# A hybrid decoder layer on one core: first block's experts handed over in two halves, weight lines read in pairs without a packed copy

## The chip, the cores and the metric

The kernel runs on one core of a Trainium2 chip. The metric is the device time of one launch in microseconds (us), as the median of several runs. Its engines are TensorE (PE, with its weight loads shown apart as PEld), VectorE (DVE), ScalarE (ACT), GpSimd (POOL) and SyncE (SP). DMAs are issued from the queues of SP (all dense loads), POOL (the gathers) and ACT (the output), and run on 16 shared DMA engines.

## What is computed

One layer on x (1024 tokens x 1024 features, f32). Three residual branches follow each other:

```python
h = rmsnorm(x, norm_mix);   x = x + hybrid_mixer(h, ...)             # MLA, RG-LRU and differential attention
h = rmsnorm(x, norm_cross); x = x + memory_cross_attention(h, rmsnorm(mem, norm_mem), w_cq, w_ckv, w_co)
h = rmsnorm(x, norm_ffn);   x = x + peer_ffn(h, peer_w_q, peer_keys, peer_u, peer_v)
return rmsnorm(x, norm_final)
```

The last branch retrieves experts. Each token has 8 heads; each head scores two sets of 128 keys, takes the 16 best of each, adds them pairwise and takes the 16 best sums. This makes 128 experts per token:

```python
act = gelu(einsum('td,thkd->thk', xt, u[et]))       # a row of peer_u (4 KB) for each token and expert
y = einsum('thk,thkd->td', gt * act, v[et])         # and a row of peer_v (4 KB)
```

So 1024 tokens x 128 experts x 2 rows x 4 KB = 1073.7 MB have to be gathered from memory.

## The kernel before

**Blocks.** The tokens are worked through in 8 blocks (0 to 7) of 128, one token per partition. A block has a front end (norm, projections, attentions, recurrence, mixer output, cross-attention, queries, key scores, choice of experts) and 128 positions of expert work. At position p VectorE multiplies the gathered `u` row of expert p with the token's h (`multiply_row`, L2052, out to `dots`), ScalarE makes the activation and a diagonal matrix of it, and TensorE sums diagonal times `v` row into `ps_sum` (L1267); every eighth `v` row is added by VectorE instead (L2074). The front end of block b runs between the positions of block b-1. Which piece stands between which positions is written in tables by hand, `TENSOR_STOPS`, `VECTOR_STOPS` and `SCALAR_STOPS`, one entry per loop body: a number is the count of positions of block b-1 that the engine issues before it goes on with that part of the piece. Each body runs once (`LOOPS`). Ahead of the bodies stands an opening: the front end of block 0, which has no expert work under it, with the projection of the memory (`mem_piece`) and the five projections of block 1 (`next_0` to `next_4`) in it.

**Gathers.** POOL issues one indirect DMA for each of the 128 experts of a block and each table: 128 rows of 4 KB, 512 KB. The `u` rows go into a ring of 9 slots and the `v` rows into another of 9 (`retrieve`, L810 and L824). The order is fixed: 12 `u` gathers, and from then on one `u` and one `v` in turn, so that a `u` gather that waits for its slot (freed by `multiply_row`) also holds the `v` gathers behind it. The first 64 expert numbers of a block are handed over by `hand_first_ids` as soon as `choose_0` has them.

**The choice** is VectorE work in four pieces: `top_0` and `choose_0` for heads 0 to 3, `top_1` and `choose_1` for heads 4 to 7 (L1931 to L1998). In the opening `next_norm` (scale x of block 1, L1724; gains on its transpose, L1742) stands between `top_0` and `choose_0`. After `choose_1` the hand-over follows: second half of the numbers (L2011), the token's h (`h_cur`, L2015, in PSUM), the gates (L2022) and x (L2031). Only then comes the first body.

**Weights.** All dense weights lie in memory as `wstream`, slices of 128 x 512 numbers, 256 KB each. SP loads them two at a time into a ring of 4 pairs (`load_pair`, L601). Partition p needs line p of both slices, so a pair is read as two lines of 2 KB per partition. While the opening runs, `pack` (L607) also copies the 49 pairs of a block from memory to memory into `packed`, where the two lines stand side by side; block 1 and the later ones read `packed`, one run of 4 KB per partition. A block needs 49 pairs. The copies stand in SP's queue ahead of the pairs of the memory projection (two copies each, 32 in all), at `cross_scores` (12) and at `top_0` (5).

**Waits on counts.** Where VectorE waits for a count that grows with the block (`wait_more`), the value comes from a register: one instruction (L583) and a register addition, which the listing of the program's order shows as `ISA` and `REGISTER_ALU`.

## Time and profile before

| | |
|---|---|
| Median of 3 runs | 3484.84 us |
| Lowest, highest | 3477.87, 3487.18 us |
| Profiled execution: span from first to last instruction | 3488.4 us (the page gives no other time for this execution) |
| Instructions | 34790 |
| PE / PEld busy | 2948.9 us (85%) / 1651.9 us (47%) |
| DVE busy | 2349.6 us (67%) |
| ACT busy | 812.5 us (23%) |
| POOL busy | 2015.7 us (58%) |
| DMA | 1345.09 MB, mean 386 GB/s |
| Share of 16 DMA engines: POOL's gathers / SP's loads | 78.1% / 20.0% |

The page cuts the span into 40 slices of 87 us. Its row `DMA` is the busy share of the 16 DMA engines in tenths, its row `GB/s` what they moved. A view by windows gives the same numbers for chosen stretches; there a share of a little over 1 stands for full. The chain of waits is the chain that ended last, in order of time. `PEclk` is the granted clock of TensorE, 1.00 for 2.4 GHz and 0.50 for 1.2 GHz.

### The profile page before, as it was taken

How to read it: one execution, taken by the hardware profiler on the slowest of the kernel's cores; microseconds unless marked ns; L12 is line 12 of the kernel's file. 1: busy time of each engine (PE TensorE's matmuls, PEld its weight loads, DVE VectorE, ACT ScalarE, POOL GpSimd, SP SyncE). 2: the span in 40 equal slices, each digit the busy share in tenths (PEclk: the TensorE clock that was granted, in tenths of full speed). 3: DMA queues.
4: the chain of work that ended last, by engine and by line, in shares of the span. 5: the costliest groups of instructions: out<-in, count | busy, mean ns of one | idle time of the engine just before them, and what ended most of it. 6: DMA issues, size and time to landing. Idle time of an engine off the chain costs nothing.

```text
span 3488.4 us, 34790 instructions
## 1 busy us (share of the span) xinstructions
PE 2948.9 (85%) x10984; PEld 1651.9 (47%) x10984; DVE 2349.6 (67%) x5893; ACT 812.5 (23%) x1915; POOL 2015.7 (58%) x2085
## 2 busy tenths in 40 slices
PE   7876898888988898889997899888998889976675
PEld 6465455544545355534554456444564445522222
DVE  6229846886588765886578765886648865596555
ACT  3111411132211421133211322114221232211111
POOL 1004755666566765666565655665556655477775
PEclk9898999999999999999999999998999999999998
DMA  7788999999999999999999999999999999999998
GB/s 279 277 274 313 408 409 409 408 409 409 409 407 406 394 409 409 408 407 382 409 409 408 392 356 409 409 409 348 359 409 409 409 355 342 385 404 410 409 409 347
DMA packets 386971, 1345.09 MB, mean 386 GB/s; under 512 B 41762, under 2 KB 44834, under 8 KB 386148
## 3 DMA queue, kind: packets, MB, share of 16 engines
q0 software_dynamic: 294912, 1073.87, 78.1%
q1 hardware_dynamic: 90724, 264.79, 20.0%
q10 hardware_dynamic: 1152, 4.19, 0.3%
q8 instruction: 90, 1.47, 0.2%
q14 instruction: 93, 0.76, 0.1%
HBM read 1332.99 MB, written 35.39 MB: 392 GB/s over the span
## 4 chain that ended last, share of the span: by engine, by line
PE 38%; DMA 30%; DVE 15%; POOL 9%; issue 6%; ACT 3%; SPq 1%; DVEq 0%; POOLq 0%; ACTq 0%
PE ps_sum L1267 18%; DMA rows<-in_peer_u,ids_u 13%; DMA rows<-in_peer_v,ids_v 10%; PE ps_p L999 5%; POOL rows L824 5%; POOL rows L810 4%; DVE rows L2052 4%; PE ps_s L1181 4%; DMA rows<-in_peer_v,ids_u 3%; DMA w_ring<-packed 3%; PE ps_s L1118 2%; PE ps_p L1126 2%; DVE feat_b L1935 1%; DVE feat_b L1931 1%; PE ps_s L1114 1%
## 5 line engine op out<-in xcount | busy, mean ns | idle before, releaser
L1267 PE MATMUL ps_sum<-rows,diag 128*128 128x512 f32 x3548 | 1727.6, 629 | 267.1 <-DMA rows<-in_peer_v,ids_v 141.4
L2052 DVE CUSTOM_DVE_ANT_0 rows<-h_cur,rows 128x1024 f32<-128x1024 f32 x1024 | 1226.8, 1220 | 496.3 <-DMA rows<-in_peer_u,ids_u 483.3
L810 POOL DMA_INDIRECT rows<-in_peer_u,ids_u x1024 | 1012.3, 989 | 702.0 <-issue 483.3
L1267 PEld LDWEIGHTS ps_sum<-rows,diag 128*128 128x128 f32 x3548 | 671.0, 200 | 1155.7 <-issue 1005.7
L824 POOL DMA_INDIRECT rows<-in_peer_v,ids_v x512 | 490.3, 958 | 433.8 <-PE ps_sum L1267 277.6
L824 POOL DMA_INDIRECT rows<-in_peer_v,ids_u x512 | 498.2, 973 | 284.7 <-PE ps_sum L1267 144.2
L1528 ACT ACTIVATE diag<-ident,acts 128x128 f32<-128x128 f32 x887 | 324.7, 394 | 1049.4 <-PE ps_sum L1267 750.1
L999 PE MATMUL ps_p<-hT,w_ring 128*128 128x128 f32 x2944 | 358.7, 282 | 28.8 <-DMA w_ring<-packed 15.3
L999 PEld LDWEIGHTS ps_p<-hT,w_ring 128*128 128x128 f32 x2944 | 353.0, 198 | 61.2 <-issue 39.7
L1834 DVE CUSTOM_DVE_ANT_0 e<-ps_s,bias_t 128x256 f32<-128x256 f32 (+6 forms) x96 | 74.2, 773 | 176.3 <-PE ps_s L1118 73.7
L2074 DVE SCALAR_TENSOR_TENSOR x_cur<-rows,acts,x_cur 128x1024 f32<-128x1024 f32 x137 | 175.6, 1282 | 7.4 <-DMA rows<-in_peer_v,ids_v 7.3
L1905 DVE TENSOR_TENSOR x_next<-x_next,ps_s 128x512 f32<-128x512 f32 x32 | 21.9, 685 | 200.0 <-PE ps_s L1181 200.0
L1516 ACT ACTIVATE acts<-dots 128x8 f32<-128x8 f32 x128 | 26.6, 208 | 486.9 <-DVE dots L2052 486.6
L1181 PE MATMUL ps_s<-w_ring,hT 128*128 128x512 f32 x256 | 118.3, 608 | 14.2 <-DMA w_ring<-packed 7.4
L1441 ACT ACTIVATE e<-e,small 128x256 f32<-128x256 f32 (+6 forms) x96 | 75.4, 785 | 219.7 <-DVE small L1836 219.4
L999 PE MATMUL ps_p<-pT,w_ring 128*128 128x128 f32 x1024 | 118.8, 276 | 0.9 <-DMA w_ring<-packed 0.9
L999 PEld LDWEIGHTS ps_p<-pT,w_ring 128*128 128x128 f32 x1024 | 116.9, 192 | 5.4 <-issue 3.3
L1181 PE MATMUL ps_s<-w_ring,feat_b 128*128 128x512 f32 x256 | 114.8, 592 | 1.1 <-DMA w_ring<-in_wstream 1.1
L1935 DVE FIND_INDEX8 feat_b<-feat_b,e 128x8 uint32<-128x128 f32 (+1 forms) x384 | 103.4, 279 | 0.0
L1118 PE MATMUL ps_s<-k_diff,feat_a 32*128 32x512 f32 (+2 forms) x192 | 83.7, 543 | 16.9 <-DVE small L1836 16.8
L1314 ACT ACTIVATE feat_a<-ps_p 128x512 f32<-128x512 f32 (+2 forms) x48 | 26.0, 542 | 304.6 <-PE ps_p L999 304.5
L2052 DVE DVE_READ_ACCUMULATOR2_ANT dots<- 128x1 f32 x1024 | 84.4, 82 | 0.0
(288 smaller groups left out, 2376.2 us busy)
## 6 DMA issues: line engine op xcount, KB each, us to landing
w_ring<-packed SPq DMA_DIRECT2D x343, 512.0 KB
w_ring<-in_wstream SPq DMA_DIRECT2D x65, 512.0 KB
packed<-in_wstream SPq DMA_DIRECT2D x49, 512.0 KB, 8.2
rows<-in_peer_u,ids_u POOLq DMA_INDIRECT x1024, 14.9
rows<-in_peer_v,ids_u POOLq DMA_INDIRECT x512, 12.6
rows<-in_peer_v,ids_v POOLq DMA_INDIRECT x512, 19.3
bias_rows<-rows SPq DMA_DIRECT2D x5, 1024.0 KB, 12.1
bias_t<-in_x SPq DMA_DIRECT2D x8, 512.0 KB, 7.9
```

The costliest lines, as they stand in the source:

```text
L810: pool.indirect_dma_start(u_rows[:, slot, :], None, peer_u, bass.IndirectOffsetOnAxis(ap=ids_u[:, j:j + 1], axis=0)).then_inc(u_landed[slo ...
L824: pool.indirect_dma_start(v_rows[:, slot, :], None, peer_v, bass.IndirectOffsetOnAxis(ap=ids[:, j:j + 1], axis=0)).then_inc(v_landed[slot] ...
L999: ins = pe.matmul(dst, w[:, k, :], lhs[:, kt, :], start=(kt == 0), stop=(kt == KT - 1))
L1118: ins = pe.matmul(ps_s[:, c0:c1], q_diff[r:r + DK, half // 4, :], k_diff[r:r + DK, half // 4, c0:c1], start=True, stop=True)
L1181: pe.matmul(ps_s[:, n * 512:(n + 1) * 512], lhs[:, kt, :], w, start=(kt == 0), stop=(kt == KT - 1)).then_inc(w_used, 1)
L1267: ins = pe.matmul(ps_sum[:, c * 512:(c + 1) * 512], diag[:, n % 4, :], v_rows[:, slot, c * 512:(c + 1) * 512], start=(j == 0), stop=(n == ...
L1441: act.activation(buf[:, 0:keys_n], buf[:, 0:keys_n], ACT.Exp, bias=small[:, 32 + n:33 + n], accum_out=small[:, 48 + n:49 + n]).then_inc(s_ ...
L1528: act.activation(diag[:, n % 4, :], ident[:, :], ACT.Copy, scale=coef[:, j:j + 1]).then_inc(diag_made, 1)
L1834: run(dve.tensor_tensor_reduce(buf[:, 0:keys_n], ps_s[:, 0:keys_n], bias[:, 0:keys_n], 1.0, -3.0e38, ALU.add, ALU.max, small[:, 16 + n:17 ...
L1935: dve.max_index(i[:, first:first + 8], v[:, first:first + 8], s).then_inc(top_step, 1)
L2052: dve.tensor_tensor_reduce(row, h_cur[:, :], row, 1.0, 0.0, ALU.mult, ALU.add, dots[:, p:p + 1]).then_inc(u_used, 1)
L2074: dve.scalar_tensor_tensor(x_cur[:, :], v_rows[:, slot, :], coef[:, j:j + 1], x_cur[:, :], ALU.mult, ALU.add)\
```

## The change

1. `pack` and `packed` are gone. `load_pair` reads `wstream` directly, but so that partition (h, q) receives lines 2q and 2q+1 of slice h: one run of 4 KB. The features of the input thereby stand in another order in the partitions (`as_given` and `as_read` are the two orders of a row of 1024). Four pairs of a block, those of the recurrence's channels (`WHOLE`), are still read as two lines of 2 KB.
2. The order of features is made where rows are written: VectorE's writes of `feat_a`, `x_next`, `x_cur`, the scaled memory and `h_cur` step through one side with a stride, in 2 or 4 instructions for one. TensorE's transposes of `xs` and its products with `mem_v` read every second column. The gains (`cols`) come in 15 small DMAs for one.
3. In the opening `next_norm` no longer stands ahead of `choose_0`; `first_choose` does choose_0, the gates of the first half, scale, h, gains of block 1 and x. `top_1` and `choose_1` of block 0 become `late_top` and `late_choose`, the first pieces of the first body.
4. The transposes and gains of the first half of a row are no longer made in the middle of the output product, but both halves after it (`norm`).
5. VectorE's waits on registers become waits on constants (`wait_for`).
6. The tables of the first body are new; in the others one stop of `mix_out` and one of `cross_out` goes.

```diff
 TENSOR_STOPS = [
-    {"latents": (1,), "mla_up": (9,), "gates": (17, 18), "recur": (20, 26), "mla_0": (29, 30, 31), "mla_1": (31, 31, 32),
...
+    {"latents": (4,), "mla_up": (10,), "gates": (17, 18), "recur": (20, 26), "mla_0": (29, 30, 33), "mla_1": (33, 33, 33),
...
 VECTOR_STOPS = [
+    {"late_top": (0, 0, 0, 0, 0, 0), "late_choose": (0, 0, 0, 0, 0, 0, 0, 0, 1, 7, 7), "latents": (7, 7), "mla_up": (9,),
...
-                dst = w_ring[:, slot_of(n), :]
-                if n < MEM_SLICES + BLOCK_SLICES:
-                    dst, src = dst.rearrange("p (s c) -> p s c", s=2), wstream[i:i + 2].rearrange("s p c -> p s c")
+                dst, src = w_ring[:, slot_of(n), :], wstream[i:i + 2]
+                if i - MEM_SLICES in WHOLE:
+
+                    dst, src = dst.rearrange("p (s c) -> p s c", s=2), src.rearrange("s p c -> p s c")
+                elif 2 * KT <= i < MEM_SLICES:
+
+                    turn = (i - 2 * KT) % KT
+                    src = wstream[i - turn:i - turn + KT].rearrange("(h k) (q s) c -> k h q (s c)", h=2, s=2)[turn // 2]
                 else:
-                    src = packed[(i - MEM_SLICES) // 2]
+                    src = src.rearrange("h (q s) c -> (h q) (s c)", s=2)
                 sp.dma_start(dst, src).then_inc(w_landed[slot_of(n)], 16)
 
-            def pack(first, last):
...
-            sp.dma_start(cols[:, :], columns).then_inc(cols_in, 16)
             sp.dma_start(x_in[:, :], x[0:P, :]).then_inc(x_landed, 16)
+            sp.dma_start(cols[:, GAINS:COL["yn"]], columns[:, GAINS:COL["yn"]]).then_inc(cols_in, 16)
+            sp.dma_start(cols[:, COL["yn"] + KT:], columns[:, COL["yn"] + KT:]).then_inc(cols_in, 16)
+            for h in range(2):
+                own = slice(h * P // 2, (h + 1) * P // 2)
+                for n in range(4):
+                    sp.dma_start(cols[own, n * KT:(n + 1) * KT].rearrange("q (s k) -> q s k", s=2),
...
+                for n in (0, KT - 2):
+                    sp.dma_start(cols[own, COL["yn"] + n:COL["yn"] + n + 2],
...
+            sp.dma_start(cols[:, COL["yn"] + 2:COL["yn"] + KT - 2], columns[:, COL["yn"] + 2:COL["yn"] + KT - 2]).then_inc(gains_in, 16)
...
-                    pack(i - 1, i + 1)
...
-            def first_next(b):
-                sp.wait_ge(first_packed, 16 * IN_TILES)
-                front_loads(1, 0, per_tile * 3)
...
-                        if n == 1 and kt == 4:
-                            turn_added(b, norm, 0)
...
                 pace.part(0.6)
-                turn_added(b, n, 1)
+                for g in range(2):
+                    turn_added(b, n, g)
...
+            def wait_for(semaphore, waited, n):
+
+                waited[0] += n
+                dve.wait_ge(semaphore, waited[0])
...
-                dve.tensor_scalar(feat_a[:, :], x_in[:, :], small[:, 7:8], None, ALU.mult).then_inc(scaled, 1)
+                for n in range(2):
+                    ins = dve.tensor_scalar(as_read(feat_a)[:, n], as_given(x_in)[:, n], small[:, 7:8], None, ALU.mult)
+                ins.then_inc(scaled, 1)
...
+            def hand_row(b, ins_of):
+
+                for n in range(2):
+                    for half in range(2):
+                        ins = dve.scalar_tensor_tensor(as_given(h_cur)[:, n, :, :, half], as_read(x_next)[:, n, :, :, half],
+                                                       small[:, 105:106], as_given(ps_s)[:, n, :, :, half], ALU.mult, ALU.mult)
+                ins_of(ins)
...
+            def first_choose():
+
+                choose(0, 0)
+                scale_x(1)
+                dve.wait_ge(consts_in, 96)
+                dve.wait_ge(pre["v_out"], 4)
+                dve.wait_ge(ffn_spread, 1)
+                hand_row(0, steps.note)
+                dve.tensor_copy(g_cur[:, 0:FIRST], g_next[:, 0:FIRST]).then_inc(g_handed, 1)
+                for g in range(2):
+                    gain_x(1, 0, g)
+                hand_x(0)
+                steps.settle(dve)
+
+            def late_choose():
+
+                choose(0, 1)
+                dve.tensor_copy(ids_u[:, FIRST:], ids_next[:, FIRST:]).then_inc(ids_handed, 1)
+                dve.tensor_copy(g_cur[:, FIRST:], g_next[:, FIRST:]).then_inc(g_handed, 1)
+                dve.wait_ge(g_handed, 2)
+                hand_last_ids(0)
+                dve.wait_ge(v_ids_handed, 1)
+                dve.nop().then_inc(handed, 1)
```

**Where instructions move, VectorE, end of the opening.** Before, behind the last part of `choose_1` (`ids_u` are the expert numbers, the row of `h_cur,rows` is one position):

```order
L1990 TENSOR_REDUCE pT<-e 128x64
L1991 SCALAR_TENSOR_TENSOR pT<-pT 128x64
L1996 TENSOR_REDUCE small<-pT 128x8
L1997 RECIPROCAL small<-small 128x8
L1998 TENSOR_TENSOR pT<-pT,small 128x128
L2011 COPY ids_u<-pT 128x64
L2015 SCALAR_TENSOR_TENSOR h_cur<-x_next,small,ps_s 128x1024
L2022 COPY g_cur<-pT 128x128
L2026 COPY ids_v<-ids_u 128x64
L2031 COPY x_cur<-x_next 128x1024
L2127 UNCONDITIONAL_BRANCH
L1754 TENSOR_TENSOR pT<-feat_a 128x384
```

Changed, behind the last part of `choose_0`; what follows the branch is `late_top`:

```order
L2040 COPY ids_u<-pT 128x64
L2033 TENSOR_REDUCE small<-pT 128x4
L2034 RECIPROCAL small<-small 128x4
L2035 TENSOR_TENSOR pT<-pT,small 128x64
L1756 TENSOR_SCALAR feat_a<-bias_t,small 128x4x64x2 x2
L2046 SCALAR_TENSOR_TENSOR h_cur<-x_next,small,ps_s 128x256 x4
L2066 COPY g_cur<-pT 128x64
L1776 TENSOR_TENSOR hT<-ps_p,cols 128x512 x2
L2095 COPY x_cur<-x_next 128x512 x2
L2192 UNCONDITIONAL_BRANCH
L1963 MAX feat_b<-e 128x8 x8
```

The hand-over of h and x stands ahead of the second half's choice, and the scale and gains of block 1 (`feat_a`, `hT`) behind the first half's numbers instead of ahead of them.

**VectorE, where the positions begin.** Changed, in the middle of `late_choose`:

```order
L2020 TENSOR_TENSOR e<-pT,iota_f 128x1024
L2023 TENSOR_TENSOR e<-e,feat_b 128x1024
L2025 TENSOR_REDUCE pT<-e 128x64
L2118 ISA rows,dots<-h_cur,rows 128x1024
L2118 ISA dots 128x1
L2020 TENSOR_TENSOR e<-pT,iota_f 128x1024
L2118 ISA rows,dots<-h_cur,rows 128x1024
```

Before position 0 stand all of `late_top` and the greater part of `late_choose`; positions 1 to 6 follow one instruction later, and the last two large instructions of the choice stand behind position 6.

**SP, where the memory projection's weights are loaded.** Before:

```order
L683 DMA bias_t<-bias_rows 128x256
L607 DMA packed<-in_wstream 256x1x512 x2
L601 DMA w_ring<-in_wstream 128x2x512
L607 DMA packed<-in_wstream 256x1x512 x2
L601 DMA w_ring<-in_wstream 128x2x512
```

Changed:

```order
L701 DMA bias_t<-bias_rows 128x256
L615 DMA w_ring<-in_wstream 128x1024 x4
L615 DMA w_ring<-in_wstream 128x1x1024 x8
L692 ISA
```

The copies are gone from between the loads, and a load has 4 KB per partition in one run.

## Rows read from the trace of the kernel before

**Rows 1.** Page, part 2 and part 6: busy share and rate in 40 slices; the copies.

```profile
DMA  7788999999999999999999999999999999999998
GB/s 279 277 274 313 408 409 409 408 409 409 409 407 406 394 409 409 408 407 382 409 409 408 392 356 409 409 409 348 359 409 409 409 355 342 385 404 410 409 409 347
...
packed<-in_wstream SPq DMA_DIRECT2D x49, 512.0 KB, 8.2
```

**Rows 2.** By windows: start:end length, busy us of PE, PEld, DVE, ACT, POOL, clock, DMA share, GB/s.

```profile
86.00:96.00 10.00, 8.68 (x43) 7.32 (x41) 4.52 (x16) 0.00 (x0) 0.00 (x0) 0.98 1.05 398
198.00:213.00 15.00, 7.86 (x42) 7.02 (x42) 2.77 (x7) 4.68 (x12) 0.00 (x0) 0.77 1.01 318
252.00:262.00 10.00, 3.42 (x15) 2.86 (x15) 8.14 (x40) 0.00 (x0) 0.00 (x0) 0.59 0.05 18
306.00:340.00 34.00, 20.00 (x52) 11.28 (x52) 30.89 (x66) 5.81 (x15) 20.77 (x22) 0.66 0.82 289
340.00:1120.00 780.00, 678.66 (x2546) 383.25 (x2547) 549.83 (x1413) 188.73 (x467) 490.88 (x505) 0.95 1.03 409
2000.00:3060.00 1060.00, 950.54 (x3620) 539.19 (x3620) 708.45 (x1742) 270.37 (x597) 617.91 (x632) 0.95 0.98 382
```

**Rows 3.** Timeline of SP's queue: start, us of issue, line, what.

```profile
0.76 0.41 SPq L610 DMA_DIRECT2D cols<-in_columns  x1
...
2.63 3.07 SPq L601 DMA_DIRECT2D w_ring<-in_wstream  x4
```

**Rows 4.** Chain of waits, start and us of a piece.

```profile
6.74 9.76 DMA xs<-in_mem
...
57.21 14.46 DMA bias_rows<-rows
...
76.04 6.41 DMA w_ring<-in_wstream
```

**Rows 5.** Timeline of PE; in brackets the idle time before and its releaser.

```profile
82.49 7.41 PE L959 MATMUL h_cur<-rows,w_ring 128*128 128x256 f32 x24 [8.15 <-DMA w_ring<-in_wstream]
...
212.61 10.54 PE L1181 MATMUL ps_s<-w_ring,feat_b 128*128 128x512 f32 x24 [1.08 <-DMA w_ring<-in_wstream]
...
260.71 23.54 PE L999 MATMUL ps_p<-hT,w_ring 128*128 128x128 f32 x192 [0.78 <-DVE hT L1742]
...
298.21 2.05 PE L1018 MATMUL ps_p<-w_ring,hT 128*128 128x128 f32 x16 [0.45 <-DMA w_ring<-packed]
```

**Rows 6.** Timeline of VectorE from the end of `top_0` to the first body.

```profile
257.15 0.75 DVE L1724 TENSOR_SCALAR feat_a<-bias_t,small 128x1024 f32<-128x1024 f32 x1
...
260.57 0.22 DVE L1958 CAST feat_b<-feat_b 128x128 f32<-128x128 uint32 x1
...
276.25 0.20 DVE L2003 COPY ids_u<-pT 128x64 uint32<-128x64 uint32 x1
276.44 1.65 DVE L1931 MAX8 feat_b<-e 128x8 f32<-128x128 f32 x8
278.21 0.09 DVE L1935 MATCH_VALUE_LOAD feat_b<-feat_b,e 128x8 f32 x1
...
297.45 1.22 DVE L1990 TENSOR_REDUCE pT<-e 128x64 f32<-128x1024 f32 x1
...
303.73 1.28 DVE L2015 SCALAR_TENSOR_TENSOR h_cur<-x_next,small,ps_s 128x1024 f32<-128x1024 f32 x1
...
306.58 1.22 DVE L2052 CUSTOM_DVE_ANT_0 rows<-h_cur,rows 128x1024 f32<-128x1024 f32 x1
```

**Rows 7.** Timeline of VectorE in the first body, behind `latents` and behind `mla_up`.

```profile
319.58 1.21 DVE L2052 CUSTOM_DVE_ANT_0 rows<-h_cur,rows 128x1024 f32<-128x1024 f32 x1
...
327.65 1.23 DVE L2052 CUSTOM_DVE_ANT_0 rows<-h_cur,rows 128x1024 f32<-128x1024 f32 x1
```

**Rows 8.** Timeline of POOL: the gather of u row 18.

```profile
331.64 0.94 POOL L810 DMA_INDIRECT rows<-in_peer_u,ids_u  x1 [0.30 <-issue]
```

More of the change, by code:

```diff
@@ L55 @@
 IN_SLICES = 2 * IN_TILES
+WHOLE = [IN_SLICES + n * KT + kt for n in range(2) for kt in (2, 4)]
+GAINS = 4 * KT
+GAIN_LOADS = 13
 CURVE = 2 * SEQ
@@ L1300, in _ @@
                     pace.start(b - 1)
-                    pace.run(stages(front, last=first == NB - 1), b)
+                    pace.run(stages(front, first, last=first == NB - 1), b)
             pace.start(NB - 1)
@@ L1564, in _ @@
                     pace.start(b - 1)
-                    pace.run(stages(front, last=first == NB - 1), b)
+                    pace.run(stages(front, first, last=first == NB - 1), b)
             pace.start(NB - 1)
```

219 lines of the change are left out of this document (116 added, 103 removed), and 5 rows, old and new, of tables (SCALAR_STOPS, VECTOR_STOPS).

## The prediction

> **What bounds the kernel now.** I read the 40 slices first [rows 1]. Behind the first four slices the rate stands at 409 GB/s nearly throughout, and the windows say the same: 409 GB/s at a DMA share of 1.03 from 340 to 1120 us, 382 GB/s from 2000 to 3060 [rows 2]. So from 340 us on the kernel runs at the pace of the 16 DMA engines, and its end is the time at which the gathers are in full flow, plus the bytes left over 409 GB/s, plus the dips. The dips lie in the attentions of the later blocks, where TensorE is busy 950.5 of 1060 us [rows 2]. Ahead of 340 us stands the opening, which the timelines show as a chain of VectorE, TensorE and single DMAs. The reader should therefore ask of every edit: does it move the start of the stream, does it change bytes or their price behind it, or does it fill a dip?
>
> The copies are 49 x 0.524 MB = 25.7 MB, 63 us of the DMA engines at 409 GB/s [rows 1]. The queue order puts all of them into the opening, ahead of the first weights of block 1. None runs where the DMA engines are the bound. So these 63 us are not on offer; what counts is the time for which the opening stood still for a DMA.
>
> **The change part by part.** All terms are against the profiled execution (3488.4 us span) and are carried over to the median of 3484.84, which lies 3.6 us lower.
>
> *Start.* 14 more small DMAs stand ahead of the first weights. Four issues took 2.63 - 0.76 = 1.87 us, 0.47 each [rows 3], so weights and memory rows are issued 6.5 us later. A part comes back, since the loads have one run per partition (the four took 3.07 us to issue, 128-line DMAs take 0.47 each: 1.2 us back), and the engines are busy less long. I take 4 us at the landing of `mem`, now 16.5 us [rows 4], plus 0.5 us for the reordered writes, so the chain of VectorE behind it is 4.5 us late. It ends in the store of the bias rows at 57.2 us [rows 4]. TensorE has 1.3 us of slack there, which leaves about +3.1 us. Bounds: 0 and +6.5.
>
> *Memory projection.* Behind that store comes the load of 6.41 us [rows 4] for which TensorE waited 8.15 us [rows 5]. Ahead of it in the queue stood two copies: 2 x 0.6 us of issue and 1.05 MB, 2.6 us at 409 GB/s. Both go: -1.3 and -2.6 us. Start and projection together: 3.1 - 3.9 = -0.8 us.
>
> *Cross-attention.* The 12 copies at `cross_scores` made the weights of `cross_out` late, but TensorE waited only 1.08 us for them at 212.6 [rows 5], because VectorE and ScalarE had been the chain until then: -1.1 us. Beyond it nothing is to be had.
>
> *Transposes behind the product.* The first half's transposes (0.44 us) go out of the product, but a transposition and a gain (0.7 us) stand behind it: +0.5 us for each of the two, +1.0 us in the opening. In the bodies TensorE has sums to do between product and transposes, so I cost it at 0. Without that cover it would be +1 us a block.
>
> *Register waits.* VectorE stood 0.12 us between MAX8 (ends 278.09) and the next row at 278.21 [rows 6], against 0.04 us behind a constant wait; 0.08 us for each of some nine in a `top` and `choose`: -0.7 us for each pair, and -0.7 us for `top_0` and the attentions of block 0. Up to the end of `top_0` the opening comes to -0.8 - 1.1 + 1.0 - 0.7 = **-1.6 us** (257.15 becomes 255.5).
>
> *First half's numbers.* `next_norm` goes from 257.15 to 260.57 [rows 6], -3.4 us, with -0.4 us of register waits: the first numbers come 5.4 us earlier, at 270.8 instead of 276.25. But only 9 u rows fit the ring, and they wait for position 0.
>
> *Up to position 0.* Before, 306.58 - 276.25 = 30.3 us. Now: gates 0.8, scale 0.9, four pieces of h 1.7, gates' copy 0.2, wait for the transposes 0.5, gains 1.5, x 0.8, branch 0.3, together 6.7; then `top_1` and `choose_1` to the end of their first wide reduction, 298.67 - 276.44 = 22.2 us [rows 6], less 0.7. This makes 28.2 us: position 0 stands at 299.0 instead of 306.6. The order shows why this isn't more: the choice is called late, but all of it except two and a half wide instructions stands ahead of position 0. The reordered one-source writes have no row. The plain one takes 0.75 us for 1024 elements [rows 6], a two-source one of h 1.28 us [rows 6]; I take 0.9, near the same instruction unordered, and keep 1.4 as the upper end.
>
> The Trainium skill (VectorE: DVE Perf Modes, What auto-detection actually checks) says that an f32 instruction with one source runs at double rate if both sides lie in SBUF and their outermost dimensions are even, whatever the step inside. By that rule the reordered writes cost 0.8 us and the sum would be 0.2 us lower; no row here has such an access.
>
> *Behind position 0.* Position 0, a wide instruction, positions 1 to 6, then the rest of the choice and the hand-over, then `latents`, which now has no position inside to cover TensorE: 1.1 + 1.3 + 6.9 + 4.2 + 0.5 + 2.5 + 6.1 = 22.6 us. Position 7 therefore stands at 321.6; before, the row behind `latents` was at 319.58 [rows 7]. `mla_up` waits for TensorE as before, so that position 9 is at 329.7 and u row 18 can be gathered at 331.0. Before it was at 331.64 [rows 8], and the stream ran without a stop from there. **Start of the stream: -0.6 us.** The 7.6 us won at position 0 are given back at `latents`.
>
> *Lines of 2 KB.* Four pairs per block, 28 in blocks 1 to 7, 14.7 MB, were 4 KB runs and are 2 KB lines now, in the stretch bound by DMA. At 2 KB lines the windows show 398 GB/s (86 to 96 us) and 318 GB/s (198 to 213 us), at shares of 1.05 and 1.01 [rows 2]. Against 409 these are +1.0 and +10.3 us. I take **+1.5 us**, near the first, since that window has no lull in it.
>
> The Trainium skill (DMA: Bandwidth & Descriptors, Why small descriptors are slow) gives a fixed overhead of about 3 cycles per packet beside 32 bytes a cycle. That makes 67 cycles for 2 KB against 131 for 4 KB, 2.3% more, an estimate of +0.8 us. It also speaks against a gain from the longer runs.
>
> *Dips.* In blocks 4 to 7 VectorE's 12 waits per block in the attentions lose 0.08 us each, 1 us a block. TensorE is the busier one there, so I count 0.6 us of it: **-2.5 us** for the four. Bounds: -6 and +2 (reordered writes, about +1.5 us of VectorE a block, which elsewhere hide behind its 483 us of waiting for u rows).
>
> Sum: -0.6 + 1.5 - 2.5 = -1.6 us, 3484.8 - 1.6 = **3483 us**. 0.3%, 10.5 us, is what a measurement of this kernel can tell from no change. The forecast is: no change. With the bounds (-3.1 and +3.4 for the start, -0.5 and +8.8 for the lines, -3.5 and +4.5 for the dips) its own range is 3474 to 3496, taking the ends as not coming together.
>
> **Rivals.** *Faster: the opening runs free of DMA waits and the start is hidden.* If small DMAs cost nothing on the chain (-3.1) and all 8.15 us at 82.5 go instead of 3.9 (-4.3), and the new table of the first body lets `mla_up` follow without its wait (-3), the stream starts 11 us earlier: 3484.8 - 11.0 + 1.5 - 2.5 = 3472.8, say 3472. For it: the rate of the second window is low, so copies may have hurt more than the waits name. Against it: SP's own start after the bias store bounds the load at 82.5.
>
> *Slower: TensorE becomes late at `latents`.* The projections of block 1 wait for `next_norm`'s gains, which go from 260.7 to about 276.5. They took 260.71 to 300.26 us [rows 5], 39.5 us with their DMA waits, and stand ahead of `latents` in TensorE's order. At 39.5 us they end at 316, and VectorE needs them at about 312. TensorE now stands still for some 20 us before them instead of 6; the granted clock over 252 to 262 us was 0.59 [rows 2], near the lower of the two levels, 1.2 GHz. If the 40 first products run at that level and the loads meet the gathers, 8 us more come on: 324, position 9 about 12 us late. It decides from 312 us on, and reaches the bound of 0.3% at about 323: 3484.8 - 0.6 + 12 + 1.5 - 1 = 3497. For it: the wait was 6 us before, and is not covered now. Against it: without waits the 272 products take 33 us (192 took 23.54 [rows 5]), and their loads are no longer behind copies.
>
> *The 2 KB lines at 318 GB/s.* 3483 + 8.8 = 3492, still within 0.3%. For it the second window, against it the first.
>
> *The choice isn't late at all.* This is so by the order of instructions, and is in the sum already. If it were late in truth, position 0 would stand 22 us earlier.
>
> **How the numbers follow.** Forecast 0.47, faster rival 0.29, slower rival 0.15, lines 0.09. Of the forecast's own chance 0.03 lie over 3495.3 and 0.02 under 3474.3; of the lines 0.03 over it. That gives faster 0.31, same 0.48, slower 0.21. The range reaches from 3467, 5 us below the faster rival, to 3499, just over the slower one.
>
> **What would show it.** Right: no `packed`; bytes 1319 MB; memory landing near 20 us; the wait at 82 us at about 4 us; position 0 near 299; position 7 near 321; the window from 340 to 1120 at 409 GB/s. Wrong: u row 18 gathered over 4 us off 331; TensorE's projections of block 1 ending behind 312 us; a rate under 406 GB/s in the same window, which would speak for the lines; or the dips from 2000 to 3060 us off 382 GB/s by over 3.

## The result

| | before | changed |
|---|---|---|
| median | 3483.91 us (4 runs, 3477.87 to 3487.18) | 3544.40 us (4 runs, 3536.28 to 3555.49) |
| profiled execution, span | 3488.4 us | 3534.3 us |
| moved in the span, mean rate | | 1319.37 MB, 373 GB/s |

The ratio is 1.0179, 95% interval 1.0151 to 1.0208: the changed kernel is 60.5 us slower. "No change", and the range of 3467 to 3499, were wrong.

### The profile after

The slices and the loads of weights on the page of the changed kernel:

```profile
DMA  7135999999999999999999999999999999999998
GB/s 243 68 128 202 354 408 409 387 408 409 409 409 408 409 402 406 404 408 407 391 409 408 409 351 401 409 408 407 335 409 409 408 374 337 409 403 410 409 409 349
...
w_ring<-in_wstream SPq DMA_DIRECT2D x408, 512.0 KB
```

Against [rows 1] the first four slices have sunk (68 and 128 GB/s in the second and third), and the fifth isn't full. From the sixth on it is the old picture. Windows of the changed kernel (length, busy us of PE, PEld, DVE, ACT, POOL, clock, DMA share, GB/s):

```profile
106.00:146.00 40.00, 26.93 (x81) 14.49 (x80) 3.21 (x15) 5.28 (x17) 0.00 (x0) 0.87 0.13 53
...
700.00:1120.00 420.00, 367.53 (x1309) 199.40 (x1308) 302.79 (x783) 100.64 (x248) 272.37 (x280) 0.94 1.03 409
...
2000.00:3060.00 1060.00, 947.25 (x3580) 533.77 (x3580) 731.88 (x1754) 286.06 (x630) 637.53 (x648) 0.96 0.99 388
```

409 GB/s stand in the steady stretch as before, and 388 against 382 GB/s in the dips [rows 2]. Up to 400 us the kernel before moved 301 GB/s and the changed one 177: 120.4 and 70.8 MB, of which 25.7 MB before were copies. The 23.9 MB that the changed kernel lacks by then are 58 us at 409 GB/s. Behind 400 us the two move 397 and 398 GB/s. So nothing was lost there, and the loss lies in the opening. The first window says where: over 40 us the DMA engines were busy for 0.13 of the time, at 53 GB/s, while TensorE did nothing for a third of it.

The chain of waits of the changed kernel, in the same place:

```profile
84.13 4.01 DMA w_ring<-in_wstream
...
98.53 48.23 DMA w_ring<-in_wstream x2
...
153.74 24.40 DMA bias_t<-bias_rows
```

and TensorE's timeline:

```profile
88.19 7.69 PE L971 MATMUL h_cur<-rows,w_ring 128*128 128x256 f32 x24 [4.44 <-DMA w_ring<-in_wstream]
...
116.86 1.98 PE L979 MATMUL ps_sum<-w_ring,rows 128*128 128x512 f32 x4 [1.59 <-DMA w_ring<-in_wstream]
126.84 3.69 PE L979 MATMUL ps_sum<-w_ring,rows 128*128 128x512 f32 x4 [5.62 <-DMA w_ring<-in_wstream]
136.82 3.51 PE L979 MATMUL ps_sum<-w_ring,rows 128*128 128x512 f32 x4 [3.13 <-DMA w_ring<-in_wstream]
146.89 3.28 PE L979 MATMUL h_cur<-w_ring,rows 128*128 128x512 f32 x4 [3.61 <-DMA w_ring<-in_wstream]
156.77 2.99 PE L979 MATMUL h_cur<-w_ring,rows 128*128 128x512 f32 x4 [3.52 <-DMA w_ring<-in_wstream]
...
178.84 1.22 PE L1131 MATMUL ps_s<-k_diff,feat_a 32*128 32x256 f32 x2 [18.32 <-DVE small L1871]
```

The wait at 82.49 [rows 5] has shrunk to 4.44 us, as forecast. But behind it is a new wait every 10.0 us: that is the time in which a pair of the memory's value weights (0.524 MB) arrives, 52 GB/s. And the bias row for the next head stands in SyncE's order behind these loads, so that it lands 24.40 us after 153.74, when attention needs it; this is TensorE's longest wait there, 18.32 us at 178.84, by way of VectorE. `mix_out` begins at 207.22, 45.8 us later than at 161.46.

What comes late a second time is at the end of the opening. VectorE of the changed kernel:

```profile
320.15 0.20 DVE L2040 COPY ids_u<-pT 128x64 uint32<-128x64 uint32 x1
...
320.98 1.20 DVE L1756 TENSOR_SCALAR feat_a<-bias_t,small 128x512 f32<-128x512 f32 x2
...
324.88 0.76 DVE L2095 COPY x_cur<-x_next 128x512 f32<-128x512 f32 x2
...
347.01 1.23 DVE L2118 CUSTOM_DVE_ANT_0 rows<-h_cur,rows 128x1024 f32<-128x1024 f32 x1
...
370.50 0.22 DVE L2033 TENSOR_REDUCE small<-pT 128x4 f32<-128x64 f32 x1 [11.48 <-ACT pT L1512]
...
388.91 1.22 DVE L2118 CUSTOM_DVE_ANT_0 rows<-h_cur,rows 128x1024 f32<-128x1024 f32 x1
```

From the first numbers to position 0 it is 26.86 us; before it was 30.33 [rows 6]. Then VectorE stands still for 11.48 us, for ScalarE's exponential of the second half's gates. ScalarE had been held by this:

```profile
368.45 0.38 ACT L1326 ACTIVATE v_diff<-ps_p 128x256 f32<-128x256 f32 x1 [16.33 <-PE ps_p L1031]
368.85 1.28 ACT L1512 ACT_TABLE_LOAD   x1
370.15 0.26 ACT L1512 ACTIVATE pT<-pT 128x64 f32<-128x64 f32 x1
```

The exponential stands in its order behind the copy of block 1's last projection. And TensorE began these projections only when `feat_a` of block 1 was scaled, which the change has moved behind the first half's choice:

```profile
322.24 1.97 PE L989 MATMUL ps_p<-ident,feat_a 128*128 128x128 f32 x8 [22.10 <-DVE feat_a L1756]
325.02 8.95 PE L1012 MATMUL ps_p<-hT,w_ring 128*128 128x128 f32 x64 [0.81 <-DVE hT L1776]
...
366.36 2.05 PE L1031 MATMUL ps_p<-w_ring,hT 128*128 128x128 f32 x16 [0.43 <-DMA w_ring<-in_wstream]
```

The tenth row (position 9, the second behind `mla_up`'s wait before, the first one in the changed kernel) is at 388.91 here and at 328.80 before: 60.1 us later, where the medians differ by 60.5. The profiled executions themselves differ by less, 45.9 us (3534.3 against 3488.4), so 14 us came back behind the tenth row in this pair; the four runs of the changed kernel are 19 us apart. That 60.1 and 60.5 agree so closely is in part luck.

### The profile page after: what moved, and what is told of

Same layout as the page of the kernel before. It is cut to its first block, busy times and chain, and to the rows that moved or that the text cites. A ratio compares the mean times of both kernels' runs of the same rounds, so it can differ in the third digit from the quotient of the medians.

```text
span 3534.3 us, 34368 instructions
## 1 busy us (share of the span) xinstructions
PE 2961.3 (84%) x10984; PEld 1659.4 (47%) x10984; DVE 2365.7 (67%) x5948; ACT 814.2 (23%) x1917; POOL 2016.8 (57%) x2085
## 2 busy tenths in 40 slices
DMA packets 371321, 1319.37 MB, mean 373 GB/s; under 512 B 42883, under 2 KB 45955, under 8 KB 370501
## 4 chain that ended last, share of the span: by engine, by line
PE 40%; DMA 28%; DVE 16%; POOL 8%; issue 5%; ACT 3%; SPq 1%; DVEq 0%; POOLq 0%; ACTq 0%
PE ps_sum L1279 18%; DMA rows<-in_peer_v,ids_v 9%; DMA rows<-in_peer_u,ids_u 9%; PE ps_p L1012 8%; DMA w_ring<-in_wstream 6%; DVE rows L2118 5%; POOL rows L836 4%; POOL rows L822 4%; PE ps_s L1191 4%; DMA rows<-in_peer_v,ids_u 3%; PE ps_s L1131 2%; PE ps_p L1139 2%; DVE feat_b L1967 1%; DVE feat_b L1963 1%; PE ps_p L1113 1%
## 5 line engine op out<-in xcount | busy, mean ns | idle before, releaser
L1938 DVE TENSOR_TENSOR x_next<-x_next,ps_s 128x512 f32<-128x512 f32 x32 | 34.3, 1073 | 219.5 <-PE ps_s L1191 219.5
L1191 PEld LDWEIGHTS ps_s<-w_ring,hT 128*128 128x128 f32 x256 | 48.0, 195 | 91.7 <-issue 49.5
## 6 DMA issues: line engine op xcount, KB each, us to landing
bias_rows<-rows SPq DMA_DIRECT2D x5, 1024.0 KB, 11.2
```

The source lines that it names most:

```text
L1191: pe.matmul(ps_s[:, n * 512:(n + 1) * 512], lhs[:, kt, :], w, start=(kt == 0), stop=(kt == KT - 1)).then_inc(w_used, 1)
```

## The experiments

My theory A: the eight loads of the memory's value weights run on two DMA engines, because the slowest dimension of their source counts 2 (the pattern takes one half-pair from two places, `k h q (s c)`). The rest of the loss is the start (the gains come in 13 small DMAs, the columns in 15) and the late gates. Rival B: the loss comes from the choice beside the rows, and the delay of the opening is of no weight. Rival C: the slow thing about the loads is their two places or their 64 partitions.

### Four kernels on the loads and the start

First kernel (e1), the weights laid side by side in memory, in the order of reading:

```diff
-                elif 2 * KT <= i < MEM_SLICES:
-                    turn = (i - 2 * KT) % KT
-                    src = wstream[i - turn:i - turn + KT].rearrange("(h k) (q s) c -> k h q (s c)", h=2, s=2)[turn // 2]
...
-    wstream = np.concatenate([column_slices(ckv[:, :D]), row_slices(ckv[:, D:]), column_slices(w_in_own), row_slices(A(w_out)[0]),
+    wstream = np.concatenate([column_slices(ckv[:, :D]), by_turn(row_slices(ckv[:, D:])), column_slices(w_in_own), row_slices(A(w_out)[0]),
```

> The changed kernel, but the memory's value weights lie in the order in which they are read, so that each of the eight pairs is one contiguous stretch and its load takes the plain path (an access pattern whose slowest dimension counts 128). Theory A (two engines): in the changed kernel these eight loads ran at about 50 GB/s and at 0.13 of the 16 DMA engines, because their slowest dimension counts 2; here they run at over 200 GB/s, mix_out begins near 167 us instead of 207, and the time falls by about 40 us, to some 3504. Rival B (the opening's delay is of no weight, the 60 us come from the choice beside the rows and from the next block's projections): mix_out moves but the stream's start hardly does, and the time stays within 10 us of 3544.

Second (e2), the changed kernel's layout, each load in two:

```diff
+                if 2 * KT <= i < MEM_SLICES:
+                    for h in range(2):
+                        sp.dma_start(dst[h * P // 2:(h + 1) * P // 2, :], src[h]).then_inc(w_landed[slot_of(n)], 16)
+                    return
                 sp.dma_start(dst, src).then_inc(w_landed[slot_of(n)], 16)
...
```

> The changed kernel with its own layout, but each of the eight loads of the memory's value weights is issued as two, of 64 partitions each: the same bytes from the same two places, only the slowest dimension counts 64 instead of 2. Theory A: as fast as with the weights laid side by side, 40 us less than the changed kernel (about 3504), DMA share in 100 to 150 us above 0.5. Rival C (what is slow is the reading of two places a megabyte apart, or writes to half of the partitions): the loads stay at 50 GB/s and the time at 3544.

Third (e3), the kernel **before** with the changed kernel's source pattern in these eight loads (the lines taken out above, put into its `load_pair`). Its features no longer match, so the experts that it chooses are not the right ones; their number and bytes are the same:

> The kernel before, with nothing changed but the source pattern of the eight loads of the memory's value weights, which becomes that of the changed kernel (slowest dimension 2; the features then don't match, only the time is of interest). Theory A: each pair takes about 10 us, the opening is longer by about 40 us and so is the whole: about 3524. Rival B: the ring of weights and the packed copies cover it, under 10 us: about 3490.

Fourth (e4), the first with the gains reordered where the columns are laid out, and one load:

```diff
-            sp.dma_start(cols[:, GAINS:COL["yn"]], columns[:, GAINS:COL["yn"]]).then_inc(cols_in, 16)
...
-            sp.dma_start(cols[:, COL["yn"] + 2:COL["yn"] + KT - 2], columns[:, COL["yn"] + 2:COL["yn"] + KT - 2]).then_inc(gains_in, 16)
+            sp.dma_start(cols[:, :], columns).then_inc(cols_in, 16)
```

> As the first of these, and the gains also come from memory in the new feature order, in the one load of the columns that the kernel before has, instead of the fifteen small ones ahead of the weights. Theory: SyncE then issues the first weights at about 3 us instead of 11.5, TensorE's first projection begins near 12 us instead of 16.9, and the time is 5 to 6 us below the first kernel here, about 3498. Rival: the delay of the start is absorbed by a later wait (for the store of the bias rows or the memory's projection), and the difference is under 2 us. What is left above the 3484 of before (some 14 us) would be the late gates and the next block's projections.

| kernel | median us | ratio to before, 95% | `mix_out` | first gather | tenth row |
|---|---|---|---|---|---|
| before | 3482.36 beside these | | 161.46 | 277.48 | 328.80 |
| changed | 3544.40 | 1.0179, 1.0151 to 1.0208 | 207.22 | 321.39 | 388.91 |
| e1 side by side | 3496.32 | 1.0050, 1.0033 to 1.0066 | 156.50 | 270.86 | 336.83 |
| e2 two halves | 3494.40 | 1.0042, 1.0027 to 1.0057 | 163.34 | 279.62 | 347.00 |
| e3 before, slow pattern | 3551.27 | 1.0213, 1.0187 to 1.0239 | 228.16 | 346.35 | 397.69 |
| e4 side by side, one load of gains | 3489.17 | 1.0022, 1.0004 to 1.0041 | 151.22 | 267.38 | 334.71 |

(The last three columns are from each kernel's profiled execution, in us.)

Laying the weights side by side takes 48.1 us off the time and 50.7 off the start of `mix_out`. Two DMAs of 64 partitions with the same bytes from the same two places do as well, so rival C falls: neither the places nor the partitions were slow. Rival B falls with them. A window of e2, over the 40 us in which the changed kernel had 0.13 and 53 GB/s:

```profile
106.00:146.00 40.00, 37.95 (x123) 20.14 (x122) 7.29 (x33) 8.72 (x31) 0.00 (x0) 0.94 0.37 102
```

and its issues of DMAs in this window (KB each, median us to landing):

```profile
w_ring<-in_wstream SPq DMA_DIRECT2D x12, 256.0 KB, 3.9
```

TensorE is busy for 38 of the 40 us instead of 27. A half load of 256 KB lands in 3.9 us, where a whole one of 512 KB took about 10. I had expected a share above 0.5 and over 200 GB/s here; these were wrong: TensorE sets the pace now, and the loads come in bursts. The profiled execution of e2 is 10 us behind that of e1 at the tenth row while the medians agree: one trace places the whole no closer than that.

The kernel before loses 69 us by this edit alone, more than I had expected, and its tenth row is 68.9 us later. TensorE of e3:

```profile
122.13 3.78 PE L970 MATMUL ps_sum<-w_ring,rows 128*128 128x512 f32 x4 [8.14 <-DMA w_ring<-in_wstream]
134.65 3.78 PE L970 MATMUL ps_sum<-w_ring,rows 128*128 128x512 f32 x4 [5.09 <-DMA w_ring<-in_wstream]
```

and its chain of waits:

```profile
98.64 23.45 DMA w_ring<-in_wstream
...
123.64 23.51 DMA w_ring<-in_wstream
```

Here a pair comes every 12.5 us; in the changed kernel, where the copies were gone, it took 10.0. If each pair's two copies spread evenly over 16 engines, the two that load also move 0.131 MB of them, and 0.655 MB at 52 GB/s are 12.5 us. That is an estimate; no run shows which engines the copies use.

53 GB/s at a share of 0.13 are two sixteenths of the steady 409 GB/s at 1.03 (51 GB/s). The Trainium skill has this rule (DMA: Bandwidth & Descriptors, Why a DMA increments its semaphore by 16 and not by 1, and Rules for kernel authors): the number of engines that a DMA uses is set by the slowest dimension that isn't 1 of its patterns, so that an outermost dimension of 2 keeps it on two. The trace agrees: 0.13 of 16 engines, and 64 as the slowest dimension restores the rate.

The gains: SyncE's queue in the changed kernel, and in e4, where the same columns come in one load:

```profile
2.15 2.59 SPq L623 DMA_DIRECT2D cols<-in_columns  x4
...
9.94 0.59 SPq L629 DMA_DIRECT2D cols<-in_columns  x1
...
11.52 1.87 SPq L615 DMA_DIRECT2D w_ring<-in_wstream  x4
```

```profile
0.76 0.40 SPq L612 DMA_DIRECT2D bias_t<-in_x  x1
1.21 0.42 SPq L613 DMA_DIRECT2D cols<-in_columns  x1
...
2.62 1.88 SPq L610 DMA_DIRECT2D w_ring<-in_wstream  x4
```

The thirteen loads of the gains take 8.4 us to issue (2.15 to 10.53), 0.64 each. Without them the first weights are asked for 8.9 us earlier, `mix_out` begins 5.3 us earlier and the whole is 7.2 us faster by the medians (3496.32 to 3489.17); the intervals of e1 and e4 overlap a little, so the size is known only roughly.

### The gains alone

The fourth edit was also made to the changed kernel by itself, with the value weights still on two engines.

> The changed kernel with only the gains in one load, the value weights still by two engines. Theory: the start and the memory's loads add up, since both stand on the same chain: 5.5 to 7 us below the changed kernel of 3544, 3537 to 3539. Rival: SyncE issues the value loads into a ring that is waited for anyway, so the earlier start is lost there: under 2 us.

3537.18 us, 1.0143 (1.0120 to 1.0166): by the medians 7.2 us below the changed kernel, as much as beside the fast loads. The two intervals overlap, though, so the times alone don't exclude the rival. In the traces `mix_out` begins at 200.14 instead of 207.22, 7.1 us earlier, the first gather is 2.8 us earlier and the tenth row, at 384.61, 4.3. That speaks for the two adding up and against a start that is lost in the ring; what reaches the end is not measured closely.

### Four kernels on the late choice

e4's first gather is 10.1 us earlier than before, and yet its tenth row is 5.9 us later. So 16 us are lost in between. First (e5), the scale and gains of block 1 ahead of the first choice again:

```diff
                 choose(0, 0)
-                scale_x(1)
...
-                for g in range(2):
-                    gain_x(1, 0, g)
...
-                     {"latents": lambda b: first_latents(), "next_norm": lambda b: None, "choose_0": lambda b: first_choose(),
+                     {"latents": lambda b: first_latents(), "choose_0": lambda b: first_choose(),
```

> The kernel with adjacent value weights and gains from one load (3489 us, 7 above before), in which VectorE scales and turns the next block's x ahead of the first choice again, as in the kernel before, instead of behind it. There, VectorE stands for 11.20 us at 316.22 for ScalarE's exponential of the late gates, which stands behind the copies of the next block's projections, which TensorE begins only after 21.26 us of idling at 268.24. Theory: TensorE begins them some 20 us earlier, the wait of 11.2 us goes, the first numbers come 3.4 us later: minus 8, about 3481. Rival: the projections are late because their weights come beside the first rows, whenever they begin; the wait stays and the time is 3489 to 3493.

Second (e6), e4 with only ScalarE's order changed (one more stop in its table goes with it):

```diff
...
+                              "next_4": lambda b: None}, 0)
...
+            def late_gates():
+                first_choose(1)
+                project_4(1)
+            front["late_choose"] = lambda b: late_gates()
```

> The same kernel of 3489 us, with only ScalarE's order changed: the exponential of the late gates stands ahead of its copy of the next block's last projection instead of behind it. Theory: VectorE's wait of 11.2 us at the gates goes, but its next step (the norm of the latents) needs TensorE's sums, and these stand behind the same last projection: the wait moves there and under 4 us are gained, 3486 to 3489. Rival: the order on ScalarE is all that costs: minus 10, about 3479.

Third (e7), both:

> Both orders changed: the next block's x ahead of the first choice, and the exponential ahead of ScalarE's last copy. Theory: as with the first alone, since the projections then end ahead of the late gates: about 3481, within 2 of it. Rival: only both together free VectorE: 3477 or less, where the first alone stays at 3485 or more.

Fourth (e8), e5 with the second half's choice ahead of all rows (and its exponential on ScalarE with it):

```diff
...
-                      "top_1": lambda b: None, "choose_1": lambda b: None}, 0)
+                      "choose_1": lambda b: late_choose()}, 0)
+            front["late_top"] = front["late_choose"] = lambda b: None
```

> The first of these (adjacent weights, one load of gains, next x ahead of the choice), and the second half of the choice stands in the opening again, ahead of the first row, as in the kernel before. Theory: the late choice buys nothing, since VectorE has the same work ahead of position 7 either way and the stream of rows flows only from there: within 4 us of the first of these, and 4 to 8 us below before (its copies, 25.8 MB of the opening's traffic, are gone and the first numbers come some 6 us earlier): 3475 to 3479. Rival: the late choice is worth the 7 positions that it lets ahead (7 of 1.15 us and the gap of the transfers): this is 8 us or more above the first of these.

| kernel | median us | ratio to before, 95% | first gather | position 0 | tenth row |
|---|---|---|---|---|---|
| before | 3483.14 beside these | | 277.48 | 306.58 | 328.80 |
| e4 | 3489.17 | 1.0022, 1.0004 to 1.0041 | 267.38 | 293.01 | 334.71 |
| e5 next x ahead | 3483.71 | 1.0006, 0.9990 to 1.0021 | 269.03 | 292.42 | 322.97 |
| e6 exponential first | 3484.81 | 1.0009, 0.9996 to 1.0022 | 270.84 | 296.46 | 332.24 |
| e7 both | 3483.95 | 1.0010, 0.9997 to 1.0022 | 271.93 | 295.32 | 325.88 |
| e8 all ahead | 3480.84 | 0.9988, 0.9976 to 1.0001 | 271.62 | 300.47 | 325.62 |

In the traces the theory holds. TensorE begins block 1's projections at 249.81 in e5 and ends them ahead of the late gates, and VectorE's wait of 11.2 us is gone; what is left for TensorE is to wait for VectorE. Of e5, TensorE:

```profile
249.81 1.97 PE L973 MATMUL ps_p<-ident,feat_a 128*128 128x128 f32 x8 [5.08 <-DVE feat_a L1740]
...
289.37 2.05 PE L1015 MATMUL ps_p<-w_ring,hT 128*128 128x128 f32 x16 [0.45 <-DMA w_ring<-in_wstream]
306.50 0.80 PE L1054 MATMUL ps_s<-pT,ones 128*128 128x128 f32 x2 [15.07 <-DVE pT L1772]
```

In e6 the wait moved, as forecast, to the latents; VectorE of e6:

```profile
318.05 0.29 DVE L1780 TENSOR_SCALAR pT<-ps_s 128x128 f32<-128x128 f32 x1 [7.56 <-PE ps_s L1056]
```

7.56 us stand there where e4 had 2.33. In time the kernels are close: e5, e6 and e7 lie 4.4 to 5.5 us below e4, with intervals that overlap with its own. So that the wait goes in e5 and only moves in e6 is shown by the traces; that the one order is worth more than the other, or how much the wait of 11 us costs at the end, is not shown by the times.

The late choice itself buys nothing: e8, with all of it ahead, has its tenth row 0.3 us earlier than e7 and 2.7 later than e5, and the lowest median. Its rival (8 us or more above e5) falls. e8 is the one version with a median below that of the kernel before: 2.3 us faster, but its interval of 0.9976 to 1.0001 still takes in no change, as those of e5, e6 and e7 do.

### The lines and the copies

The kernel before without its copies (e9), every block's weights from where the first block's are, in 2 KB lines:

```diff
-                if n < MEM_SLICES + BLOCK_SLICES:
-                    dst, src = dst.rearrange("p (s c) -> p s c", s=2), wstream[i:i + 2].rearrange("s p c -> p s c")
-                else:
-                    src = packed[(i - MEM_SLICES) // 2]
+                dst, src = dst.rearrange("p (s c) -> p s c", s=2), wstream[i:i + 2].rearrange("s p c -> p s c")
```

> The kernel before with its fifty packed copies left out, and every later block's weights read from where the first block's are, in 2 KB lines in the old feature order. Theory (the copies delayed the opening, the lines cost little): TensorE's wait of 8.15 us at 82.49 in the memory's projection shrinks to about 3, mix_out begins some 6 us earlier, the first numbers at about 270 instead of 276; position 7, which VectorE's own work sets, 2 to 6 earlier; lines of 2 KB give back 1 to 10 over 92% of the span: 3477 to 3486. Rival: 2 KB lines lower the rate of the steady stretch (409 GB/s in 700 to 1100 us) by 2%: 60 us, 3540.

And e8 with 2 KB lines for all 49 pairs of a block, where the change has them for four (the expectation has the counts wrong). Here too the features don't match, and the experts chosen are not the right ones:

```diff
-                if i - MEM_SLICES in WHOLE:
+                if i >= MEM_SLICES:
```

> The kernel in which all is chosen ahead (3481 us), with every block's weights in 2 KB lines instead of two loads in thirty-three a block (the feature order then doesn't match for the others; only the time is of interest). This measures the lines alone. Theory: under 0.3% (3481 to 3491), since each line is half as long but the rate in the steady stretch is set by the rows' 4 KB and by the sum of bytes. Rival: 31 more pairs of 0.5 MB a block at 318 instead of 409 GB/s, 0.36 us each, over 7 blocks: up to 80 us slower, 3560.

e9 took 3511.01 us, 1.0073 (1.0049 to 1.0096); e10 3507.81 us, 1.0068 (1.0046 to 1.0089). Both theories were too low and both rivals too high. The opening of e9 did as forecast: the wait at 82.49 [rows 5] is 3.96 us at 79.13, `mix_out` begins at 153.36 (8.1 us earlier), the first gather is at 270.28 and the tenth row at 324.15, 4.7 us earlier. The 27 us were lost behind it. Windows of e8 (first line) and of e10:

```profile
400.00:2000.00 1600.00, 1398.85 (x5285) 788.61 (x5284) 1144.13 (x2897) 392.12 (x933) 996.52 (x1019) 0.95 1.02 405
```

```profile
400.00:2000.00 1600.00, 1388.14 (x5236) 776.97 (x5235) 1127.69 (x2875) 387.09 (x924) 985.84 (x1010) 0.96 1.03 401
```

The share is nearly the same and the rate 1% lower. In the same window the kernel before moves 406 GB/s and e9, whose experts are the right ones, 401. By the ratios e10 is 0.80% or 27.9 us above e8, give or take 9. Its tenth row is 3.9 us later, which leaves 24 us behind the opening. The pairs that differ there are 45 a block in seven blocks, 315: 0.076 us a pair. The 28 pairs that the change reads so therefore cost 2.1 us, an estimate from this slope.

The Trainium skill (DMA: Bandwidth & Descriptors, Why small descriptors are slow) would make 2.3% of these 315 pairs: 165 MB, 404 us at 409 GB/s, an estimate of 9 us. Some 24 were measured, give or take 9, so here the rule is too low, by a factor of 1.6 to 3.6. What else is in it no run here shows.

So the packing was worth its place: by one trace each it costs 4.7 us up to the tenth row, and by the medians it gives some 32 behind it. The changed kernel's way of 4 KB runs without copies has both, if it is free of the other losses; that is e8.

### More rows ahead

```diff
-    {"late_top": (0, 0, 0, 0, 0, 0), "late_choose": (0, 0, 0, 0, 0, 0, 0, 0, 1, 7, 7), "latents": (7, 7), "mla_up": (9,),
+    {"late_top": (0, 0, 0, 0, 0, 0), "late_choose": (0, 0, 0, 0, 0, 0, 0, 0, 1, 7, 7), "latents": (12, 12), "mla_up": (14,),
```

> The kernel with all chosen ahead (3481 us), in which VectorE takes 12 rows instead of 7 ahead of the next block's latents (its norm and up-projection shift behind them). Sixteen rows have been asked for by then; GpSimd stood 3.34 and 3.39 us at 319.02 and 327.12 waiting for VectorE, and in 300 to 340 us the DMA engines were busy for 0.85 of the time or less. Theory (the whole time follows the moment from which rows flow without a gap): 3 to 6 us earlier there and in the whole, 3475 to 3478. Rival: the next block's own chain (latents, attention) moves 6 us later and its first block becomes the bound: 3481 to 3487.

3483.94 us, 1.0001 (0.9988 to 1.0013): the rival's time. The tenth row is at 307.44, 18.2 us earlier than in e8 (3.3 of them by an earlier first gather, at which the two kernels don't differ), and nothing comes of it. GpSimd of e12:

```profile
332.06 0.94 POOL L820 DMA_INDIRECT rows<-in_peer_v,ids_u  x1 [5.16 <-PE ps_sum L1263]
```

It no longer waits for VectorE there (3.34 and 3.39 us in e8) but for TensorE's sums. The windows 300 to 340 and 340 to 400 show 332 and 395 GB/s, where e8 has 297 and 408: 37.0 MB against 36.4, 1.5 us at 409 GB/s. So the tenth row tells the time only as long as its order against the next block's work stays as it is; the bytes moved by 400 us are the better measure here.

## Why the prediction was wrong

| term | forecast us | measured us | by |
|---|---|---|---|
| start and memory projection | -0.8 | +5.7 | TensorE, 82.49 to 88.19 |
| value weights, not in the sum | 0 | +40.1 more | `mix_out` +45.8; e1 -48.1 |
| cross-attention to first numbers | -4.6 | -1.9 | 112.93 against 114.79 |
| first numbers to position 0 | -2.1 | -3.5 | 26.86 against 30.33 |
| position 0 to the row behind `latents` | 22.6 long | 33.8 long | 347.01 to 380.83 |
| lines | +1.5 | +2.1, estimate | e10 |
| steady stretch | 409 GB/s | 409 GB/s | window |

Position 0 was thus 40.4 us late (347.01 against 306.58). From there to the tenth row it took 41.9 us, against 22.2 before and 30.7 in the forecast. The 8.5 us between these two the forecast had; the 11.2 us above it are the wait for the late gates.

**What failed first is the step "Memory projection".** It counted what stood ahead of the load at 82 us, got that wait right (about 4 us forecast, 4.44 measured; e2 has 4.47 there, but e1, with the same start, 0.65), and then went on to cross-attention. The eight loads behind it were taken as loads like the others. Their shape stood in the order of instructions, `128x1x1024` where the others have `128x1024`, and the diff shows `k h q (s c)` indexed by `k`, so that `h`, of 2, is outermost. I had also cited the page of the Trainium skill that gives the rule, for its figure on descriptors, and didn't weigh this load by it. No row of the trace before has such a load; the prediction bounded the other operations without a row, but not this one. One line, "0.524 MB on an unknown number of engines", would have given a bound: on 2 of 16 a pair takes 10 us, eight pairs 80 us, where TensorE before went through these weights from 105.20 to 158.11, in 52.9 us. In the changed kernel it took from 111.06 to 203.15, 92.1 us.

**Start.** 14 DMAs at 0.47 us were 6.5 us; the weights were asked for 8.9 us later (2.63 to 11.52), since a DMA of reordered gains takes 0.64 us to issue. The memory landed at 23.12 (ScalarE's first square of it) where 20 was forecast, and the two terms together came to +5.7, not -0.8. By the medians of e4 and of e11 it is 7.2 us of the whole, known only roughly. The upper bound of +6.5 was about right; the value taken was not.

**Copies.** Their removal was taken as -3.9 us in the memory projection and -1.1 in cross-attention. In e9 the product behind the first wait begins 3.4 us earlier (79.13 against 82.49), so the first figure was about right. `mix_out` is 8.1 us earlier, but the further 4.7 us are no DMA wait: from the first value weights to `mix_out` TensorE's waits for other engines sum to 6.8 us before and 7.2 us in e9, none is for a DMA, and its granted clock is 0.82 before and 0.92 in e9. The profiles of e1, e2, e4, e6 and e8, without copies too, have 0.92 there, and e5 has 0.89. Whether the copies or the longer wait ahead lower the clock, or this one execution did, no run shows. The same 4.7 us are most of the reason why `mix_out` of e1 moves by 50.7 us though it was only 45.8 late.

**The step "Behind position 0" failed second, and the rival "TensorE becomes late at `latents`" was right in its mechanism**; it was given 0.15. It forecast about 12 us; VectorE's wait is 11.48 us, and part of that agreement is luck. The projections take 43.4 us from 325.02 to 368.41, against 39.5 [rows 5]: of the 8 us that the rival added for clock and loads, 3.9 came. Even without them the prediction had TensorE end at 316 and VectorE need it at 312, and yet put no wait in its sum. The rival missed which step waits: not VectorE's latents but, ahead of them, the late gates, whose exponential stands in ScalarE's order behind the copy of the last projection. The forecast's own 22.6 us had no wait in this place; with 11.5 it is 34.1, and 33.8 were measured.

**Norms.** The transposes behind the product were taken as +0.5 us each. From the start of `mix_out` to that of `cross_q` it is 19.55 us against 17.41: +2.1 for one, four times as much. The product itself, the wait for its weights (0.21 us) and the reordered adds are in it: TensorE waits 1.16 us for the last add, against 0.78 before. I didn't take it apart by a run.

**Bounds.** The prediction's own bounds, added up, give 3476 to 3500; that its range began at 3474 doesn't follow from them. The measured 3544 lies far outside either.

**What held.** The copies' 63 us of DMA weren't on offer; the steady stretch is unchanged; the lines are cheap as the change has them; the choice is late in name only, and e8 shows that it buys nothing. The dips gave more than forecast: 388 against 382 GB/s over 1060 us, though where each kernel's blocks lie in this window has moved by 60 us.

## What to carry to other kernels

Of a DMA whose pattern the change rewrites, count the engines before the bytes: name the outermost dimension, and where it is small, price the load with that many engines. Only 2 was measured here, against 64 and 128. If a load has to gather from two places, issue two DMAs with many partitions outermost, or lay the bytes side by side ahead of time. When an engine's work is moved back to bring another's forward, look in the order of every third engine for what stands behind it: here ScalarE's copies came late by VectorE's move and held VectorE itself. And a milestone of one engine stands for the end only as long as the order around it is the same.

## What the runs showed of the hardware

- A load of 0.524 MB, 4 KB a partition, whose outermost dimension counted 2 took 10.0 us in the changed kernel and 12.5 us beside the packed copies; as two loads of 64 partitions, each half landed in 3.9 us.
- VectorE's reordered writes. By line, with min, median and max of the duration (ns), of the changed kernel:

```profile
L1750 DVE COPY x_next<-bias_t x16: 625/637/697, 8.6 to 2836.7; 128x512 f32<-128x512 f32 x16
...
L1756 DVE TENSOR_SCALAR feat_a<-bias_t,small x16: 664/684/732, 7.6 to 2689.0; 128x512 f32<-128x512 f32 x16
...
L2095 DVE COPY x_cur<-x_next x16: 410/424/656, 324.9 to 3227.7; 128x512 f32<-128x512 f32 x16
```

The first two write with the order changed (neighbouring elements 2 KB apart), the third reads so and writes in order. As copies, 512 elements take 637 ns written so and 424 ns read so; 1024 in plain order took 685 ns before. So here the reordered read costs little or nothing, and the reordered write some 210 ns a piece. The rule that the prediction cited (the Trainium skill, VectorE: DVE Perf Modes, What auto-detection actually checks) would give both the double rate; here the write of `feat_a` took 1.20 us in two pieces, where the forecast had 0.9 and the rule 0.8.
- The add of the output product, which reads and writes `x_next` in the changed order, pays the most; before and changed, from the two pages:

```profile
L1905 DVE TENSOR_TENSOR x_next<-x_next,ps_s 128x512 f32<-128x512 f32 x32 | 21.9, 685 | 200.0 <-PE ps_s L1181 200.0
```

```profile
L1938 DVE TENSOR_TENSOR x_next<-x_next,ps_s 128x512 f32<-128x512 f32 x32 | 34.3, 1073 | 219.5 <-PE ps_s L1191 219.5
```

The forecast had about +1.5 us of VectorE a block for all reordered writes; a block's four adds alone are +1.6.
- Weights in 2 KB instead of 4 KB lines lowered the rate of a stream that is otherwise 4 KB rows from 405 to 401 GB/s (400 to 2000 us, e8 and e10), at shares of 1.02 and 1.03.
